# Grouped attention: the low-part product one tile later, and VectorE's low parts behind the maxima and one tile later

## The reference

```
def attend(qblk):
    s = jnp.einsum('bkgqd,bksd->bkgqs', qblk, kh)
    p = jax.nn.softmax(s, axis=-1)
    return jnp.einsum('bkgqs,bksd->bkgqd', p, vh)
```

## Time and profile before

| what | value |
|---|---|
| median of the runs | 3721.38 us |
| profiled execution, its own time | 3719.32 us |
| span of that execution, first to last instruction | 3717.5 us |
| mean granted TensorE clock, share of full | 0.993 |
| TensorE, matmul busy | 97% of the span |
| VectorE, ScalarE, GpSimd busy | 63%, 55%, 35% |

### The profile page before, as it was taken

One profiled execution on the slowest core, in us unless ns is written; L12 is line 12 of the kernel. 1 busy time (PEld: TensorE's weight loads), 2 busy tenths in 40 slices (PEclk: granted clock), 3 DMA queues, 4 the chain that ended last, 5 costly groups with the idle time before them and its releaser, 6 DMA issues. The chain is left out here.

```text
span 3717.5 us, 57038 instructions
## 1 busy us (share of the span) xinstructions
PE 3602.0 (97%) x19930; PEld 3254.5 (88%) x19930; DVE 2327.6 (63%) x4441; ACT 2045.6 (55%) x4197; POOL 1308.8 (35%) x1018
## 2 busy tenths in 40 slices
PE   8999999999999999999989999999999999999998
PEld 8999999999987777777789999999999777777677
DVE  5243345628768888877652333466287688888776
ACT  5233344732258888776452333447232588887764
POOL 0000023003347777755400000230032477777554
PEclk9999999999999999999989999999999999999999
DMA  4455446237631121036444444463377211210354
GB/s 151 142 143 159 138 137 204 85 101 215 192 89 35 32 71 34 22 98 189 142 160 124 132 142 138 138 202 87 99 220 198 78 35 32 71 35 21 108 182 144
DMA packets 441758, 439.27 MB, mean 118 GB/s; under 512 B 98144, under 2 KB 385920, under 8 KB 438400
## 3 DMA queue, kind: packets, MB, share of 16 engines
q1 hardware_dynamic: 441184, 434.58, 38.8%
q10 hardware_dynamic: 288, 1.05, 0.1%
HBM read 292.10 MB, written 133.96 MB: 115 GB/s over the span
## 5 line engine op out<-in xcount | busy, mean ns | idle before, releaser
L792 PE MATMUL pj_acc<-h_hi,pj_whi 128*128 128x384 f32 x2880 | 1000.2, 347 | 9.9 <-DVE h_lo L1236 4.6
L792 PE MATMUL pj_acc<-h_hi,pj_wlo 128*128 128x384 f32 x2880 | 967.1, 336 | 0.0
L792 PE MATMUL pj_acc<-h_lo,pj_whi 128*128 128x384 f32 x2880 | 964.9, 335 | 0.0
L2258 POOL TENSOR_TENSOR ga_plo<-ga_prob,ga_phi 128x512 fp32r<-128x512 f32 (+1 forms) x594 | 772.4, 1313 | 418.8 <-ACT ga_prob L2186 397.8
L2291 DVE TENSOR_REDUCE pl_mx<-ga_ps_x 128x1 f32<-128x512 f32 (+1 forms) x760 | 511.1, 679 | 141.1 <-PE ga_ps_x L2114 128.5
L2184 ACT ACTIVATE ga_phi<-ga_ps_s 128x512 fp32r<-128x512 f32 (+1 forms) x792 | 470.0, 593 | 182.3 <-PE ga_ps_s L2131 176.3
L792 PEld LDWEIGHTS pj_acc<-h_hi,pj_whi 128*128 128x128 f32 x2880 | 542.8, 188 | 15.2 <-DVE h_lo L1236 5.1
L792 PEld LDWEIGHTS pj_acc<-h_lo,pj_whi 128*128 128x128 f32 x2880 | 542.9, 188 | 3.5
L792 PEld LDWEIGHTS pj_acc<-h_hi,pj_wlo 128*128 128x128 f32 x2880 | 541.9, 188 | 0.0
L2186 ACT ACTIVATE ga_prob<-ga_ps_s 128x512 f32<-128x512 f32 (+1 forms) x792 | 466.3, 589 | 22.0 <-DVE ga_plo L2258 18.2
L1539 POOL TENSOR_TENSOR rq_sqlo<-rq_sq,rq_sqhi 128x384 fp32r<-128x384 f32 x48 | 50.2, 1046 | 1132.3 <-ACT rq_sqhi L1082 1127.2
(11 more groups left out here) (245 smaller groups left out, 6685.8 us busy)
## 6 DMA issues: line engine op xcount, KB each, us to landing
pj_w<-in_w_in SPq DMA_DIRECT2D x62, 512.0 KB, 4.0
dl_kv<-dil_kv SPq DMA_DIRECT2D x108, 256.0 KB, 2.9
proj<-pj_ring SPq DMA_DIRECT2D x132, 192.0 KB, 2.8
fi_z<-proj SPq DMA_DIRECT2D x36, 640.0 KB
rq_trig<-in_trig SPq DMA_DIRECT2D x48, 384.0 KB, 3.3
gqk<-rq_parts SPq DMA_DIRECT2D x48, 384.0 KB, 3.0
ml_qk<-mqk SPq DMA_DIRECT2D x144, 128.0 KB, 2.8
ml_mb<-gate_M SPq DMA_DIRECT2D x72, 256.0 KB, 3.6
```

The source lines that it names most:

```text
L792: mm = pe.matmul(acc[s % 2][:, 0:CHUNK], wt[u][:, t, :], ht[:, t, tok], start=(t == 0 and i == 0), stop=(t == KT - 1 and i == 2))
L2258: vector.tensor_tensor(p_lo[r][:, 0:w], prob[f % 2][:, 0:w], p_hi[r][:, 0:w].bitcast(F32), ALU.subtract).then_inc(sem, 1)
```

## The change

In TensorE's stream the third product of a tile leaves `weigh` and becomes `weigh_low`. Step f is now: scores of tile f, the maximum product, the low product of tile f - 3, the two high products of tile f - 2. Behind the last step the remaining ones follow in the old order. In VectorE's stream the low part of its own tiles is made in the step two behind its tile, no longer one, and behind the step's maximum instead of ahead of it. As `pv_done` of an item's last tile now comes one step later, `finishing` starts three (prompt: seven) steps behind an item's end, and VectorE's loop is one step longer. No buffer, semaphore or arithmetic changes.

```
--- before.py
+++ after.py
@@ -2133,12 +2133,17 @@
             def weigh(f):
                 o, kt = TILES[f]
                 g, u, w, r = ITEMS[o][0] // GQ_PER_KV, bank(o), width(o), f % 4
-                first, last = f == FIRST[o], f + 1 == FIRST[o + 1]
+                first = f == FIRST[o]
                 if first:
                     past(pe, o_ok, NI, before_in_bank(o))
                 past(pe, phi_ok, NTILE, f + 1)
                 pe.matmul(ps_o[u][:, 0:w], v_hi[g][:, key_tile(f), :], p_hi[r][:, 0:w], start=first, stop=False)
                 pe.matmul(ps_o[u][:, 0:w], v_lo[g][:, key_tile(f), :], p_hi[r][:, 0:w], start=False, stop=False)
+
+            def weigh_low(f):
+                o = TILES[f][0]
+                g, u, w, r = ITEMS[o][0] // GQ_PER_KV, bank(o), width(o), f % 4
+                last = f + 1 == FIRST[o + 1]
                 low_ready(pe, f)
                 pe.matmul(ps_o[u][:, 0:w], v_hi[g][:, key_tile(f), :], p_lo[r][:, 0:w], start=False, stop=last).then_inc(pv_done, 1)
 
@@ -2156,6 +2161,8 @@
                 if f == 2:
                     past(pe, fill, NFILL, 5)
                     past(pe, fill_v, NFILLV, NFILLQ + 1)
+                if f >= 3:
+                    weigh_low(f - 3)
                 if f >= 2:
                     weigh(f - 2)
                 for o in rows_at(f):
@@ -2166,8 +2173,10 @@
                 if f == TURNED_AT + 7:
                     past(pe, row_ok, NI, NI)
                     turn_heads(0)
-            weigh(NTILE - 2)
-            weigh(NTILE - 1)
+            weigh_low(NTILE - 3)
+            for f in (NTILE - 2, NTILE - 1):
+                weigh(f)
+                weigh_low(f)
             past(pe, exped, NTILE, NTILE)
             past(pe, wlo_ok, WEIGHTS, WEIGHTS)
             slot(0)
@@ -2318,7 +2327,7 @@
             def finishing(f):
 
                 for o in range(NI):
-                    since = f - FIRST[o + 1] - (6 if ITEMS[o][2] else 2)
+                    since = f - FIRST[o + 1] - (7 if ITEMS[o][2] else 3)
                     if 0 <= since < pieces(o):
                         reciprocal(o, since)
                         if since == pieces(o) - 1:
@@ -2334,13 +2343,13 @@
             for c in range(2, NQC + 1):
                 nc.vector.memset(q_lom[c][HD:P, :].bitcast(F32), 0.0).then_inc(fill_v, 1)
             past(dve, fill_v, NFILLV, NFILLQ + 1)
-            for f in range(NTILE + 12):
-                if 1 <= f <= NTILE and by_dve(f - 1):
-                    low_half(dve, nc.vector, f - 1, plo_dve)
+            for f in range(NTILE + 13):
                 if f == SECOND_AT[2] + 4:
                     values_low(1, 8)
                 for m in maxes_at(f):
                     maximum(m)
+                if 2 <= f < NTILE + 2 and by_dve(f - 2):
+                    low_half(dve, nc.vector, f - 2, plo_dve)
                 finishing(f)
                 if f in LOG_SIGMOIDS:
                     log_sigmoid(LOG_SIGMOIDS[f])
```

## The result

The changed kernel takes 3830.6 us (median of four runs, 3827.9 to 3831.4) against 3721.3 us: 1.029 of the time before, 95% interval 1.028 to 1.031, **slower by 109 us** where 65 were forecast.

What follows compares the result with a forecast made beforehand. TensorE, busy 97% of the span, was taken as the bound. From 3719.3 us, 111 us added (55 + 18 + 12 + 18 + 8) and 46 removed gave +65: 3784 us, range 3735 to 3820.

Steps and rivals of the forecast that it cites:

- the collision: VectorE's low part meets GpSimd's of the next tile and ends 0.06 to 0.23 us later; 0.09 taken, 18 us.
- the pieces of w_out_lo: GpSimd's 32 pieces push its next low part 0.5 us into VectorE's; half counted, 8 us.
- VectorE's surplus: Reciprocals and divisions on VectorE delay low parts that have no slack: 12 us at wide items, 18 at prompt items.
- what is removed: TensorE's old waits for low parts and maxima, 29 and 7 us, and slow restarts, 10 us: 46 us removed.
- The mechanism: VectorE's low part moves back two maxima, TensorE's use only 0.90 us, so the product is late in 198 tiles.
- Rival 1: Faster: TensorE's waits go and no new ones come, 3673 us; chance 0.08.
- rival 2: A draw: 0.28 us per VectorE tile comes, but GpSimd's meeting and VectorE's extra work cost nothing, 3728 us; chance 0.12.
- Rival 3: Slower still: ScalarE becomes the bound behind the low parts, its second exponential 1.1 us late, 3811 us; chance 0.23.
- covered by 0.3 us: ScalarE's delayed second exponential would end at 2.34 us, scores want it at 2.64, so its wait costs nothing.
- The chain in itself: Maximum, low part, weight load take 1.77 us against 1.59: 0.18 late plus 0.10 restart, 198 tiles, 55 us.
- I take 0.09, near the lower end: Delay per VectorE tile from meeting GpSimd's low part, picked from 0.06 to 0.23 us, expecting GpSimd to start at once.
- today's slack takes about 1: Of 2.5 us of prompt items' reciprocals and division on VectorE, about 1 us is hidden; 12 x 1.5 = 18 us.

Runs made afterwards that it cites:

- e3: Changed kernel with TensorE's part undone (all three products of tile f-2 in step f again), VectorE's part kept: 3987.4 us, ratio 1.0719.
- e13: Changed kernel with the maximum product ahead of the scores, and GpSimd's next low part waiting for VectorE's: 3755.2 us, ratio 1.0086.
- e14: Changed kernel with maximum product before scores, GpSimd's next low part waiting for VectorE's, and reciprocals spread over steps without VectorE low parts: 3707.6 us, ratio 0.9957.
- e4: Changed kernel with the low product of tile f-3 behind the two high products of tile f-2 in TensorE's step: 3820.1 us, ratio 1.0270.
- e5: Changed kernel with GpSimd's low part behind a VectorE tile waiting until VectorE's low part is done: 3800.9 us, ratio 1.0224.

## Why the prediction was wrong: the chain held, three terms of the sum did not

The forecast of 65 us fell 44 short. The steps that failed are the sizes of three terms: the collision (26 us with the pieces of w_out_lo, measured 36), VectorE's surplus (30, measured 45) and what is removed (46, measured 31). That makes 40 of the 44. The range was too narrow for the same reason. Its upper end, 3820, moved the collision and the pieces alone; the surplus had no end of its own in it, and the end that the text did give for the removed waits ("nothing") was not carried into it.

- **The mechanism** (low part behind the maximum of step t+2, wanted one step and one product later) was right, link by link: 0.43, 0.60, 0.05 us and a wait in nearly every tile, 184 of 198. e3, e13 and e14 show it by its size. Rival 1 (the waits go and none comes) and rival 2 (a draw) fell with that. Rival 3, ScalarE as the bound, did not come: the scores wait 19.1 us for it (11.7 before). But it was close: "covered by 0.3 us" was too much. It put the collision's 0.09 into the start of the scores and not into the end of the exponential; with it on both sides 0.2 is left, and in the tile above the exponential ends at 1271.74 and the scores start at 1271.98. e4 shows that 0.46 us later at the low product is enough to have the scores wait.
- **The chain in itself**, 0.28 us per tile or 55 us, was sized right: the shortest late tiles lose 0.16 to 0.20 us and a restart of 0.11.
- **The collision** was under-sized. The step took 0.09 us for each tile and 8 us for the pieces of w_out_lo, 26 us. Over the 180 wide tiles whose low part stands behind a maximum on VectorE, low parts last 36 us longer than 0.68 us each, 0.20 on average. I had counted on GpSimd's part starting on time; where ScalarE or GpSimd is late with it, VectorE's ends up to 1.1 us later, and most of it is paid (e5 took 30 us back). The rows had the bound, 0.23 us, near which the average came, and the sum took the lower end.
- **VectorE's surplus** was under-sized: 12 + 18 us forecast, 41 us measured as the start of the maximum later than 0.43 us after its product, and 4 us more for the joined maxima (0.17 us) that stand between maximum and low part and that the count left out. This is what the surplus costs after the change, not what the change adds by it: spreading the reciprocals gave the changed kernel 31 us and the kernel before 26.
- **What is removed** was over-sized: 46 us forecast; of the 77 us that TensorE lost before, 46 are left besides VectorE's low parts and their restarts, 31 went. VectorE's low parts had cost 24 us (23 by the forecast's rule) and the maxima gave 7 (7), but GpSimd's low parts gave 2 (6) and the restarts behind the three gave 6 (10). Against these 39 some 8 us are new: 4 at the scores and 4 at the products of line 1875 near the stage's end.

The terms come to 136 us; counted on TensorE, 140 us were added (117 and 23) and 31 removed, 109 in place of the 65 that 111 and 46 gave. So the stages took 1255.5 us where some 1212 were said, and the waits for VectorE's low parts were 0.88 us each where about 0.4 was said. The forecast's step "I take 0.09, near the lower end" and the step "today's slack takes about 1" share a fault: with no slack left at the low product, the mean delay counts, not the usual one.

On the restart, the table in the Trainium skill's TensorE: Matmul & The Clock Gate would have weight loads pulled ahead of matmuls in flight. The trace doesn't show it for a load whose product waits: in the tile above the load starts at 1271.16, when the low part is done, and the next product comes 0.34 us behind. On the collision, the skill's SBUF — State Buffer (Summary: rules for kernel authors) says that, where a VectorE instruction has two SBUF inputs and a GpSimd one reads SBUF, the second to issue blocks until the first has finished. The trace of the changed kernel agrees but for some 0.13 us: in the first stage GpSimd's low part began first in all 70 cases in which the two overlapped, and VectorE's, 0.68 us long by itself, ended 0.55 us behind GpSimd's end (median).

## What to carry to other kernels

When a producer and its consumer are both moved back, count the distance for each engine in its own order: here VectorE's low part moved behind two more maxima, TensorE's use by 0.90 us only. A product with no slack pays every delay of the engines ahead of it in full, so price the mean of the delays (collisions, surplus work) and not the usual case, and let the range hold the ends of every term. And when waits for one engine vanish at one place, look whether that engine has the time: until VectorE's reciprocals were spread, the same waits came back at the maxima.

## What the runs showed of the hardware that had not been expected

Where GpSimd's low part began first, the end of the VectorE low part that met it was set by GpSimd's end: 0.55 us behind it, whether VectorE's began 0.36 us or 1.04 us after GpSimd's (lasting 1.48 and 0.80 us). Starting it earlier made it longer by as much. Where VectorE's began first, as in 23 cases of the first stage of the kernel before, it was the other way round: GpSimd's ended 1.15 us behind VectorE's (median) and lasted up to 1.81 us in place of 1.29. A late weight load on TensorE costs 0.11 us beyond its own lateness, in each such tile.
